# A hybrid decoder layer on one core: the expert block written anew, with gathers of 32 tokens x 4 slots

## The reference, cut to what matters

```python
h = rms_norm(x, norm_pre_ffn) * (1.0 + scale2) + shift2          # after x += gate1 * rms_norm(mixers @ w_out)
qry = (h @ w_query).reshape(T, 8, 2, 128)                        # 8 heads, 2 sides
sub_scores = einsum('thpd,hpnd->thpn', qry, sub_keys)            # 128 keys a side
top_s, top_i = top_k(sub_scores, 16)                             # 16 of each side
cand_s = top_s[:, :, 0, :, None] + top_s[:, :, 1, None, :]       # 256 pairs
best_s, best_pos = top_k(cand_s, 16)                             # 16 experts a head, of 16384
gates = softmax(best_s)
act = gelu(einsum('td,thkd->thk', h, u_table[expert_idx]))       # 128 rows of U a token
y = einsum('thk,thkd->td', gates * act, v_table[expert_idx])     # 128 rows of V a token
x = x + gate2 * rms_norm(y, norm_post_ffn)
```

## Time and profile before

| what | value |
|---|---|
| runs of the kernel before, median | 4292.56 us |
| span of the profiled execution | 4370.2 us |
| start of `peer_block` in the profile (its first load) | 926.55 us |
| first product with a gathered U tile | 1019.68 us |
| first `finish` | 1444.10 us |
| last `finish` | 4360.56 us |
| PE, DVE, ACT, POOL busy over the span | 76%, 58%, 22%, 61% |
| moved over the whole span | 1184.53 MB |

### The profile page before, as it was taken

The page is one execution under the profiler, slowest core; times in us unless marked ns, Lnnn a source line. Parts: engine busy times, 40 slices in busy tenths (PEclk is TensorE's granted clock), DMA queues, the critical chain, the costliest instruction groups (busy, mean ns, idle before and its releaser), DMA issues.

```text
span 4370.2 us, 44073 instructions
## 1 busy us (share of the span) xinstructions
PE 3333.3 (76%) x9929; PEld 1731.2 (40%) x9944; DVE 2548.4 (58%) x5725; ACT 961.4 (22%) x1993; POOL 2665.9 (61%) x2467
## 2 busy tenths in 40 slices
PE   6998999977777767777677677767777677777676
PEld 5775888854222322232233222323332233222232
DVE  5786656635555565556655655565556556555654
ACT  4232444432111111112111111111111111111111
POOL 2233322205777677767776777777777767777776
PEclk9999999989999999999999999999999999999998
DMA  4323111138889898989989999999998889898998
GB/s 178 133 100 116 43 58 58 38 135 288 320 320 329 318 327 317 331 315 327 323 318 325 326 331 322 326 326 339 317 330 318 314 320 330 319 324 319 332 339 293
DMA packets 334937, 1184.53 MB, mean 271 GB/s; under 512 B 36944, under 2 KB 51728, under 8 KB 330640
## 3 DMA queue, kind: packets, MB, share of 16 engines
q0 software_dynamic: 297984, 1084.36, 69.2%
q1 hardware_dynamic: 36880, 99.45, 6.3%
HBM read 1168.98 MB, written 14.68 MB: 271 GB/s over the span
## 4 chain that ended last, share of the span: by engine, by line
issue 23%; DMA 19%; POOL 19%; PE 14%; DVE 2%; POOLq 1%; ACT 1%; another core or an unknown queue 0%; SPq 0%; DVEq 0%; ACTq 0%
DMA vr<-in_v,vidx 16%; PE ps_acc L1178 10%; POOL vr L1015 9%; POOL ur L1010 8%; DMA ur<-in_u,uidx 2%; PE ps_y L1149 2%; PE ps_sc L1164 2%; DVE ur L1323 1%; POOL vidx L1003 1%; POOL uidx L1003 1%; DMA ur<-in_gain_post_ffn 0%; POOLq L1003 0%; PE ps_acc L1194 0%; POOLq L1008 0%
## 5 line engine op out<-in xcount | busy, mean ns | idle before, releaser
L1178 PE MATMUL ps_acc<-vr,diag 128*128 128x512 f32 x4096 | 2095.4, 642 | 888.8 <-DMA vr<-in_v,vidx 712.5
L1178 PEld LDWEIGHTS ps_acc<-vr,diag 128*128 128x128 f32 x4096 | 742.3, 199 | 2215.2 <-issue 1766.6
L1323 DVE SCALAR_TENSOR_TENSOR ur<-ur,h2c 128x1024 f32<-128x1024 f32 x1024 | 1205.5, 1223 | 497.5 <-DMA ur<-in_u,uidx 465.0
L1015 POOL DMA_INDIRECT vr<-in_v,vidx x1024 | 1138.1, 1111 | 487.2 <-issue 301.1
L1010 POOL DMA_INDIRECT ur<-in_u,uidx x1024 | 1148.5, 1122 | 401.2 <-issue 260.5
L1075 ACT ACTIVATE diag<-ident,coef 128x128 f32<-128x128 f32 x1024 | 370.8, 396 | 1486.8 <-PE ps_acc L1178 703.9
L1315 DVE RECIPROCAL esum<-esum 128x1 f32<-128x1 f32 x64 | 10.5, 163 | 588.1 <-ACT ex L1067 404.3
L1071 ACT ACTIVATE gel<-gel 128x8 f32<-128x8 f32 x128 | 26.6, 208 | 1139.8 <-DVE gel L1330 985.8
L1164 PE MATMUL ps_sc<-Wk,h2T 128*128 (+1 forms) x1024 | 245.7, 395 | 15.4 <-ACT h2T L1063 10.8
L1164 PEld LDWEIGHTS ps_sc<-Wk,h2T 128*128 128x128 f32 x1024 | 203.1, 200 | 71.3 <-issue 42.8
L589 POOL CAST wh<-wt 128x1024 fp32r<-128x1024 f32 x32 | 38.2, 1192 | 304.2 <-PE ps_b L64 161.7
(11 more groups left out here) (272 smaller groups left out, 3895.0 us busy)
## 6 DMA issues: line engine op xcount, KB each, us to landing
ada<-in_w_ada SPq DMA_DIRECT2D x24, 1024.0 KB, 5.5
wt<-in_w_head SPq DMA_DIRECT2D x32, 512.0 KB, 3.5
ur<-in_u,uidx POOLq DMA_INDIRECT x1024
vr<-in_v,vidx POOLq DMA_INDIRECT x1024
wt<-in_w_lru SPq DMA_DIRECT2D x27, 512.0 KB, 9.2
vr<-in_wqT SPq DMA_DIRECT2D x16, 512.0 KB, 5.3
xt<-in_x POOLq DMA_DIRECT2D x8, 512.0 KB, 5.1
merged_scratch<-lru POOLq DMA_DIRECT2D x8, 512.0 KB, 2.9
```

Of the source, the lines that this page charges most:

```text
L1015: pool.indirect_dma_start(vr[:, r % VR], None, a["v"], bass.IndirectOffsetOnAxis(ap=vidx[:, par, r:r + 1], axis=0)).then_inc(v_in[r % VR], 16)
L1178: last = nc.tensor.matmul(ps_acc[:, half(s)], diag[:, r % ND], vr[:, r % VR, half(s)], start=False, stop=False, skip_group_check=True)
L1323: last = v.scalar_tensor_tensor(ur[:, r], ur[:, r], 1.0, h2c[:], ALU.mult, ALU.mult, accum_out=dots[:, r:r + 1])
```

## The change

The expert block is rewritten.

- **Gathers.** A round R takes 4 slots. Gather b of a round (b = 0 to 3) fetches, for tokens 32b to 32b+31, their 4 slots: token 32b+i and slot s stand in partition 32s+i. There are still 128 rows to a gather, 4 gathers of U and 4 of V to a round, 32 rounds to a tile. U has 8 buffers and V 12. Indices and gates are spread into that layout by ACT (`spread_half`, 16 copies for half a tile); DVE converts the indices (`indices`) once for half a tile. U and V gathers read the same index columns.
- **U products.** The h rows that go with the layout (`h2r`, four blocks, each token four times) come from a DRAM copy of h by four loads, each to 32 partitions.
- **V products.** A coefficient column becomes a 128x32 stack of four 32x32 diagonals (`stacks`, from `mask`), and PE multiplies it into 32 rows of `ps_acc`: for each half of the columns four products follow each other, into four row blocks. `start` and `stop` stand in the first and last round; the zero products go.
- **Tables.** Wk is written to DRAM at the start, and for every tile Wk (8 blocks of 1 MB) and `w_out` (4 blocks of 1 MB) are loaded again through 3 buffers (`wb`) from SP's queue. x2 and h go to DRAM and come back.
- **Order.** All loops are written out, and all waits compare with constants; the `go` increments are gone. The next tile's work stands at fixed rounds (`next_tile`). All 8 heads of tile 0 are selected before its first product; each later tile's selection falls into the rounds of the tile before.
- In `gated_linear_attention` the semaphores are cleared and freed at its end, behind a barrier of all engines.

The core of the diff:

```diff
+    wk_dram, h2_dram, x2_dram = ...   # DRAM scratch: (PH, P, 2 * D), (TC, P, D), (TC, P, D)
-    R = 8
-    GROUPS = TOPK // R
-    VR = ND = 4
+    NU, NV = 8, 12
+    ROUNDS = SLOTS // 4
+    WB, Q = 3, 256
+    QUARTERS = D // Q
+    BLOCKS = QUARTERS + PH
...
         def _(sp):
+            def store_wk(h):
+                sp.wait_ge(key_out, 2 * h + 2)
+                sp.dma_start(wk_dram[h], wk_stage(h)).then_inc(wk_stored, 16)
+            def load_block(t, i):
+                n = BLOCKS * t + i
+                if n >= WB:
+                    sp.wait_ge(wb_used, n - WB + 1)
+                if i < QUARTERS:
+                    sp.dma_start(wb[:, n % WB], a["w_out"][:, :, i * Q:(i + 1) * Q]).then_inc(wb_in[n % WB], 16)
+                else:
+                    if t == 0:
+                        sp.wait_ge(wk_stored, 16 * (i - QUARTERS + 1))
+                    sp.dma_start(wb[:, n % WB].rearrange("p k n -> p (k n)"), wk_dram[i - QUARTERS]).then_inc(wb_in[n % WB], 16)
+            def spread_rows(t):
+                sp.wait_ge(h2_stored, 16 * (t + 1))
+                if t >= 2:
+                    sp.wait_ge(dots_done, SLOTS * (t - 1))
+                for s in range(4):
+                    sp.dma_start(h2r[32 * s:32 * s + 32, t % 2], h2_dram[t].rearrange("(b i) d -> i b d", b=4)).then_inc(h2r_in[t % 2], 16)
...
         def _(pool):
-            with pool.Fori(0, TC * PH - 1) as H:
-                both(2 * H, 0)
-                pool.wait_ge(sel_ready, H + 2)
-                both(2 * H + 1, 1)
+            def gather_u(R, b):
+                t, r, n = R // ROUNDS, R % ROUNDS, 4 * R + b
+                if b == 0 and r % (ROUNDS // 2) == 0:
+                    pool.wait_ge(uidx_ready, R // (ROUNDS // 2) + 1)
+                if n >= NU:
+                    pool.wait_ge(dots_done, n - NU + 1)
+                pool.indirect_dma_start(ur[:, n % NU], None, a["u"], bass.IndirectOffsetOnAxis(ap=uidx[:, t % 2, b, r:r + 1], axis=0)).then_inc(u_in[n % NU], 16)
+            def gather_v(R, b):
+                if n >= NV:
+                    pool.wait_ge(v_used, (n - NV) // 4 + 1)
+                pool.indirect_dma_start(vr[:, n % NV], None, a["v"], ...).then_inc(v_in[n % NV], 16)
+            for R in range(ROUNDS * TC):
+                for b in range(4):
+                    if R + 1 < ROUNDS * TC:
+                        gather_u(R + 1, b)
+                    gather_v(R, b)
...
         def _(act):
-            act.sem_inc(diag_out, R)
+            def stacks(R):
+                act.wait_ge(coef_ready, R + 1)
+                if R >= 2:
+                    act.wait_ge(v_used, R - 1)
+                for b in range(4):
+                    S.activation(stack[:, R % 2, b], mask[:], ACT.Copy, scale=coef[:, R % 2, b:b + 1]).then_inc(stack_out, 1)
+            for t in range(TC):
+                for r in range(ROUNDS):
+                    R = ROUNDS * t + r
+                    if R > 0:
+                        stacks(R - 1)
+                    if r == 0 and t > 0:
+                        finish(t - 1)
+                    if t + 1 < TC:
+                        next_tile(t + 1, r)
+                    tanh(R)
...
         def _(pe):
+            def mix(R):
+                r = R % ROUNDS
+                pe.wait_ge(stack_out, 4 * (R + 1))
+                for b in range(4):
+                    n = 4 * R + b
+                    pe.wait_ge(v_in[n % NV], 16 * (n // NV + 1))
                 for s in range(2):
+                    for b in range(4):
+                        last = nc.tensor.matmul(ps_acc[32 * b:32 * b + 32, half(s)], stack[:, R % 2, b], vr[:, (4 * R + b) % NV, half(s)], start=(r == 0), stop=(r == ROUNDS - 1), skip_group_check=True)
+                last.then_inc(v_used, 1)
+            def next_tile(t, r):
+                if r < 2:
+                    mixed(t, 2 * r)
+                    mixed(t, 2 * r + 1)
+                if r == 4:
+                    turn(t)
+                if r >= 6 and r % 3 == 0 and r < 30:
+                    scores(t, r // 3 - 2)
...
         def _(dve):
+            def products(t, r):
+                R = ROUNDS * t + r
+                for b in range(4):
+                    n = 4 * R + b
+                    dve.wait_ge(u_in[n % NU], 16 * (n // NU + 1))
+                    v.scalar_tensor_tensor(ur[:, n % NU], ur[:, n % NU], 1.0, h2r[:, t % 2, b], ALU.mult, ALU.mult, accum_out=dots[:, R % 2, b:b + 1]).then_inc(dots_done, 1)
+            for r in range(2, ROUNDS):
+                next_tile(0, r)
+            for t in range(TC):
+                for r in range(ROUNDS):
+                    products(t, r)
+                    coefficients(t, r)
+                    if r == 1 and t > 0:
+                        finish(t - 1)
+                    if t + 1 < TC:
+                        next_tile(t + 1, r)
```

More of the change, by code:

```diff
@@ L1135, in _ @@
-            with act.Fori(PH * (TC - 1), PH * TC - 2) as H:
-                head(H)
-            for H in range(PH * TC - 2, PH * TC):
-                head(H, select=False)
+            def next_tile(t, r):
+                if r == 2:
+                    mixer_norm(t)
+                if r == 3:
+                    expert_norm(t)
+                if r == 5:
+                    turned(t)
+                if r >= 9 and r % 3 == 0:
+                    weights(t, r // 3 - 3)
+                if r == 19:
+                    spread_half(t, 0)
+                if r == 31:
+                    spread_half(t, 1)
@@ L1226, in _ @@
-            pe.wait_ge(acc_out, TC - 1)
-            edge(True)
-            with pe.Fori(0, PH - 2) as h:
-                scores(PH * (TC - 1) + h + 2, TC - 1, h + 2)
-                head(PH * (TC - 1) + h)
-            for H in range(PH * TC - 2, PH * TC):
-                head(H)
-            edge(False).then_inc(acc_done, 1)
+                    last = nc.tensor.matmul(ps_sc[:, 0:2 * NK], h2T[:, k], wb[:, n % WB, k], start=(k == 0), stop=(k == KC - 1))
+                last.then_inc(wb_used, 1)
@@ new lines, in next_tile @@
+            def next_tile(t, r):
+                if r < 2:
[5 more added lines that the diff above has]
+                    scores(t, r // 3 - 2)
+            mixed(0, 0)
+            mixed(0, 1)
+            for g in range(2):
+                keys(g)
+            mixed(0, 2)
+            mixed(0, 3)
+            for g in range(2, KEYS):
+                keys(g)
@@ L1362, in _ @@
-            mixer_norm(0)
-            expert_norm(0)
-            for n in range(2):
-                select_sides(n)
-                select_pairs(n)
-            dve.wait_ge(h2_copied, 1)
-            alone()
-            products(0)
-            with dve.Fori(0, TC - 1) as t:
-                step.loop(t, PH * HEAD_STEPS + 2)
-                for first, last in ((0, 3), (3, 5), (5, PH - 1)):
-                    with dve.Fori(first, last) as h:
-                        step.loop(h - first, HEAD_STEPS)
-                        head(PH * t + h)
-                    step.end(last - first)
-                    if first == 0:
-                        mixer_norm(t + 1)
-                    if first == 3:
-                        expert_norm(t + 1)
-                head(PH * t + PH - 1, take=t + 1)
-                finish(t)
@@ L1383, in _, with next_tile @@
-            step.end(TC - 1)
-            with dve.Fori(0, PH - 2) as h:
-                step.loop(h, HEAD_STEPS)
-                head(PH * (TC - 1) + h)
-            step.end(PH - 2)
-            for H in range(PH * TC - 2, PH * TC):
-                head(H, select=False, more=H < PH * TC - 1)
+            def next_tile(t, r):
+                if r == 2:
+                    mixer_norm(t)
+                if r == 3:
+                    expert_norm(t)
+                if r >= 7 and r % 3 == 1 and r < 31:
+                    select_sides(t, r // 3 - 2)
+                if r >= 8 and r % 3 == 2:
+                    select_pairs(t, r // 3 - 2)
+                if r >= 9 and r % 3 == 0:
+                    select_experts(t, r // 3 - 3)
+                if r == 19:
+                    indices(t, 0)
+                if r == 31:
+                    indices(t, 1)
```

519 lines of the change are left out of this document (245 added, 274 removed).

## The result

The changed kernel takes 4128.57 us (median of 4 runs, 4122.87 to 4129.56) against 4295.11 us (4285.42 to 4300.59) for the kernel before on the same chip: a ratio of 0.9611, 95% interval [0.9593, 0.9629], or 167 us less. Forecast were 4107 us. The profiled execution took 4128.46 us with a span of 4126.9. Of the nine runs of the kernel before on the third chip of the experiments one took 17925.52 us; it is left out of the ratios and medians given there.

A forecast was written before the change was run, and what follows sets the result against it. POOL's full queue was taken to bound the kernel, then POOL and DMA nearly level. 7 x 385 + 368 = 3063 against 3340.9 us gives -278; with +87 and +2, -189, scaled -186: 4107 us, range 3970 to 4400.

The forecast's parts named there:

- The gap of 0.30 us: POOL's queue: the 0.30 us before each gather (77 us a tile) stays when increments and register waits go; gain 0.
- rival C: POOL's queue: the gap goes too, only bytes bound at 416 GB/s, 365 us a tile; 3927 us in all, chance 0.12.
- POOL at 366 us a tile: POOL's queue: 256 gathers of 0.94 us, plus 0.19 lost to DVE products and 0.30 of gap each.
- Bytes at 406 GB/s, 374 us: DMA transfers: 152.0 MB a tile, where the kernel before has 135.8, taken at 406 GB/s, 374 us.
- A: DMA: byte ceiling, a full share moves only 358 GB/s, 425 us a tile; slower, 4392 us, chance 0.22.
- B: POOL and DMA: the old stalls (27 us) stay, 401 us a tile; 4234 us in all, chance 0.17.
- The 11 us of stalls: POOL and DMA combined: a tile taken as 385 us, a third of the way from 374 (perfect decoupling) to 401.
- the sentence on the rule: h2r loads: 32 partitions reach 8 of 16 ports, so 11 us a tile instead of 5, forecast 42 us later; not summed.
- D: Gathers locked out: half begin inside DVE product runs and take 1.97 us, POOL 449 us a tile; 4628 us, chance 0.05.
- E: PE: row blocks serial and at the low clock, 604 us a tile; over 5000 us in all, chance 0.02.
- The start: Before the first product: eight heads selected first, so first product at 1112 instead of 1019.7, +92 us, bounds +70 to +115.
- the -5 and +2 of the small terms: Start and end: -5 us for 12 gathers out instead of 8 by the first product, +2 for barrier and longer last round.

The follow-up runs named there:

- e9: The kernel before with one of its two index copies dropped, V's gathers reading U's copy: 4318.92 us against 4352.0 beside it, ratio 0.9927.
- e1: The changed kernel with each gather fetching only the first 2 KB of each 4 KB row: 4153.93 us, ratio to the kernel before 0.9565.
- e7: The changed kernel with 4 V buffers instead of 12: 6075.94 us, ratio to the kernel before 1.4152.
- e4: The changed kernel with all four V products going to rows 0 to 31, so they can't run at once: 4210.21 us, ratio to the kernel before 0.9694.

## Why the prediction was right

The direction was right, and the cause given for it: POOL's queue was full, it lost its copies and its waits for V buffers, and a tile fell from 416.6 to 384 us. The total, 4107 against 4128.57, and the tile, 385 against 383.9, are both close, and both partly by luck: the total because two errors cancelled, the tile because the 11 us put in for stalls had the right size and another kind.

*POOL's queue full before.* The copies and the V buffers were the lever, but not as a plain sum: in e9 a third of the freed time came back. How the gain divides between the two isn't shown; no run gave the kernel before more V buffers.

*The gap of 0.30 us is the gather's own.* Right, and rival C with it wrong: 0.28 to 0.30 in every kernel, with increments and registers or without.

*POOL at 366 us a tile.* Right for the changed kernel (363), wrong as a constant. The loss to DVE's products, taken as 0.19 us, is 0.18 in full tiles, 0.05 in the last and 0.23 in e1: I take it to depend on where the gathers fall against the products, which no run tests. The last tile, lines of 3800 to 4100 us:

```profile
L1070 POOL DMA_INDIRECT ur<-in_u,uidx x116 | 120.6, 1039 | 35.3 <-issue 35.3
L1076 POOL DMA_INDIRECT vr<-in_v,uidx x116 | 109.5, 944 | 35.4 <-issue 35.4
```

256 x (0.99 + 0.30) = 330 us: the forecast 368 is the term that was mis-sized, by 40 us to the good. POOL waits for nothing there, and the bytes at 409 GB/s are level with it.

*Bytes at 406 GB/s, 374 us.* 152 MB in 383.9 us are 396 GB/s at a share of 1.02. So A, a ceiling of 358, is wrong: the share rose from 0.90 to 1.02 and the rate from 322 to 396 GB/s, by more than the share. B, 401 us, is wrong too: waits for PE went from 27 to 1.2 us a tile, as twelve V buffers were to do, and e7 shows what four would have meant in the new layout.

*The 11 us of stalls, "a third of the way".* They were taken as left-overs of the old waits. What stands there is new: 17 us of waits for U buffers on top of POOL's 368. About 5 come from the late `w_out` block. The prediction had looked at the table loads and put them at nothing ("one block per three rounds ... so they come in time"), which holds for the blocks of Wk and not for the four of `w_out` in two rounds; and the path that it named for a late block, through the V buffers with 35 us of cover, isn't the one that was taken, through ACT's norm, the tanh and the U buffers. Some 7 come in the hole of the h2r loads, which the prediction had priced in the sentence on the rule and left out of its sum. D, gathers locked out at 1.4 us, is wrong by the mean of 1.117; E by e4's clock. PE works 155 to 158 us in a full tile, between the 107 and the 214 us forecast for overlapped blocks at the two clocks, DVE 254 (277): off the path, as said, but for the late block.

*The start.* 1112 forecast, 1117.73 measured. The tiles after it: first product to first `finish` 378.7 us, forecast 385.

Summed up on the profiled spans: forecast 4370.2 - 189 = 4181, measured 4126.9, so the sizes were 54 us too high: last tile 40, the six before it 17, the stretch up to the first `finish` 6, against 9 too few at the start (6 us later, and the -5 and +2 of the small terms), which makes 54. Then I scaled 4181 by 0.982 to 4107, as if the changed kernel's profile too would stand 1.8% above its runs. It stands at its median (4128.46 and 4128.57), so the scaling took 74 us too many. The two errors nearly cancelled, and 22 us are left. For the same reason the two traces differ by 243 us where the medians differ by 167. The profiled execution of before was a long one of its kernel. A part of it may be the "remote" waits, 25.5 + 3.0 us in 7.2 tiles, of which the changed kernel's trace has none; the rest isn't known.

## What to carry to other kernels

Where two resources are each within 5% of the tile's time, easing one returns almost nothing; test them together before either is called the bound (within 6 us of 384 apart, 42 off together). Read the DMA share and the rate side by side: the share of 1.03 at 254 GB/s came with loads into few partitions, and only windows as short as the load show it. Buffers that are freed in groups must be counted in groups. Count streamed blocks against the rounds in which they are used, not against the tile's mean, and follow a late one through every in-order queue behind it.
